# Mixer's first chunks in another order, S5 tables on POOL, the last branch rows kept in SBUF, and routing with one scan

## The chip, the cores and the metric

The kernel runs on one core of a Trainium2 chip. Time is that of the device, in microseconds (us), from the start to the end of one execution. An engine name in the text is PE (matrix products), DVE (vector), ACT (activation functions), POOL (GpSimd) or SP (it issues most DMAs).

## What is computed

One decoder layer on 2048 tokens of 1024 features: a normalisation, a mixer of four causal branches that are merged with gates, a residual, a second normalisation, a mixture of experts (32 experts in 4 groups, two per token), a residual and a last normalisation.

```python
def hybrid_mixer(xn, w_in, ...):
    proj = xn @ w_in                                   # 2048 x 1792
    ya = short_conv_mixer(a_b, a_c, a_x, conv_a_w)     # bg * conv3(cg * xv)
    yb = pool_mixer(p_u, pool_w, pool_b, pool_scale)   # window means of 2, 4, 8, 16 tokens, then a product
    yc = s5_mixer(s_u, ...)                            # h_t = a h_(t-1) + B u_t, complex; gelu; glu
    yd = rglru_mixer(l_x, l_g, ...)                    # conv4, two gates, h_t = a_t h_(t-1) + b_t
    branch = jnp.einsum('bskw,kwd->bskd', stack(ya, yb, yc, yd), branch_w)
    gates = jax.nn.sigmoid(xn @ merge_gate_w + merge_gate_b)
    return jnp.sum(gates * branch, axis=2) @ w_out

def hier_moe(xn, ...):
    # softmax over 4 groups, best group; the two best of its 8 experts; their softmax times the group's value
    # tokens sorted by expert, blocks of rows per expert
    h = jax.nn.silu(xb @ w1[e]) * (xb @ w3[e])
    return h @ w2[e]                                   # weighted, added to the token's row

def reference(x, ...):
    h = x + hybrid_mixer(rms_norm(x, norm1_g), ...)
    h = h + hier_moe(rms_norm(h, norm2_g), ...)
    return rms_norm(h, final_norm_g)
```

## The kernel before

Every large product is made from splits: a float32 operand is written as a high part (`_hi`, by ACT) and a low part (`_lo`, by DVE or POOL), and three matmuls per tile take hi·hi, lo·hi and hi·lo. The program runs in stages: mixer (`mix_branches`), merge (`merge_branches`), routing (`route`), experts (`run_experts`), and the final sum (`combine`). Within a stage each engine has its own list of instructions written out by hand in the order in which it runs; engines wait for one another on semaphores. There is no scheduler. What an engine does next is what stands next in its list, so an instruction that waits holds up all behind it.

**Mixer.** Four chunks of 512 tokens. For each, ACT squares and scales the rows of x (`squares`, `scale_rows`), DVE computes the inverse root by Newton steps in between (`rms_scale`, which calls `rsqrt_steps`), PE transposes (`first_tiles`), ACT and DVE write the two halves of the transposed x (`x_highs`, `x_lows`). Then fourteen projection tiles (`tile(c, i)`) of 24 matmuls give the inputs of the branches, in the order of `F_ORDER`. The two PSUM rings `gr` (emptied by ACT, `evac`) and `dr` (emptied by DVE) hold the tiles' results and those of the small products: `gates` (the block-diagonal gates of the RG-LRU branch, on `xc` of `lru_conv`), `pool_out` (on the pooled rows of `pool_mix`; `pool_result` empties it), `states_in` and `states_out` (the S5 branch: input to states, states to output), and `glu`. DVE's pieces are `lru_conv`, `gate_poly`, `lru_squares`, `lru_out`, `conv_a(c, j)` (the short convolution), `states(c, u)`, `y_poly`, `y_gelu`, `carry_states` and `glu_out`. The buffer `late` holds in chunk 0 the raw weights `raw` and later the states and the S5 output; so `tile(2, 0)`'s loads and the store of a branch go through SP's one queue.

In chunk 0 w_in is also split: SP loads a raw tile, ACT writes `win_hi` and POOL `win_lo`, and both are spilled to DRAM (`w_in_parts`) to be loaded in the later chunks. The rows of `u` make a round trip through DRAM (`turn_u`, on POOL) to `u4`. DVE prepares parameters during that time (lines 988 to 1110; the semaphore `masks_set` closes it), POOL then builds tables of cosines and sines by doubling (lines 439 to 450), and DVE the powers of the S5 matrices (lines 1124 to 1138), which PE transposes into Toeplitz tables.

At its end SP stores the chunk's four branches and x to DRAM. **Merge** loops over four trips of 512 tokens, and the last chunk comes first: `load_piece` and `load_x_parts` load branches and x again. SP loads for the next trip after the current one is split. `load_merge_weights` brings one set of weights per branch.

**Routing.** On DVE: softmaxes, one-hot marks (`oh`, `hot`) of the chosen experts, counts by PE (`tri`, `ones`), running sums over the 16 token tiles, blocks per expert, positions (`pos`), and the table of tokens for each block (`table`). Beside it POOL splits expert 0's weights into low parts (lines 1776 and 1781 of `ExpertWeights`).

**Experts.** For each block of tokens POOL gathers rows (`gather`), PE transposes them, and the three products follow. Weights of the next expert are loaded by SP, split into high parts by ACT and low parts by DVE and POOL while the current expert runs.

## Time and profile before

| | |
|---|---|
| time, median of 3 runs | 2833.48 us (2831.18 to 2833.7) |
| profiled execution | 2833.71 us |
| its span in the profile | 2832.1 us |
| PE busy / DVE / ACT / POOL | 2423.3 / 1457.3 / 1034.9 / 563.8 us |
| mixer | 0 to about 570 us |
| merge | about 570 to 1768 |
| routing | 1768 to about 1847 |
| experts | 1847 to about 2700, then the sum |

The profiled execution took 1.6 us more than its span, that is time around the first and last instruction. Busy time is summed over instructions; a stage in which PE is busy most of the time is bound by matmul work, a stage in which it is not is bound by what PE waits for. In a timeline row the bracket holds how long the engine was idle before the group, and who released it: an engine and line, or a DMA by its tensors, where "DVEq" or "SPq" is the engine's sequencer. In a window row the busy times of PE, PE's weight loads, DVE, ACT and POOL stand in this order.

### The profile page before, as it was taken

To read this page: it belongs to the slowest core of one execution; us is meant where nothing else is said; L and a number is where in the kernel's file an instruction comes from. 1 tells how busy PE (TensorE), PEld (TensorE's weight loads), DVE (VectorE), ACT (ScalarE), POOL (GpSimd) and SP (SyncE) were. 2 spreads that over 40 slices of the span, in tenths; PEclk is the share of its full clock that TensorE was granted. 3 is DMA by queue.
4 is the path that set the end of the run, shared out by engine and by line. 5 is a ranking of instruction groups with operands and counts; after the bars stand their busy time and mean duration, and the time that the engine had idled before them with its cause. 6 is when DMAs were issued, how large, how long until landed. Compare 5 with 4: busy or idle time off the path is not lost. (4 is left out here: it accounts for less than half of the span.)

```text
span 2832.1 us, 36678 instructions
## 1 busy us (share of the span) xinstructions
PE 2423.3 (86%) x11820; PEld 1866.0 (66%) x11821; DVE 1457.3 (51%) x2190; ACT 1034.9 (37%) x1254; POOL 563.8 (20%) x436
## 2 busy tenths in 40 slices
PE   6678698879999999999999999189999999998930
PEld 5466476668857886688758875167777667777730
DVE  6777366533333343334334333846456564665648
ACT  4322232222222222122212221146556565666621
POOL 3501001000000000000000000434334443345451
PEclk9889899989999999899999998589999999999975
DMA  8653456564463446244624452277777777788866
GB/s 251 250 190 115 164 201 244 156 210 136 129 208 100 125 142 209 81 143 135 209 90 134 129 185 107 90 257 297 265 270 286 276 255 267 276 308 319 295 259 282
DMA packets 385018, 569.61 MB, mean 201 GB/s; under 512 B 34896, under 2 KB 218448, under 8 KB 384976
## 3 DMA queue, kind: packets, MB, share of 16 engines
q1 hardware_dynamic: 348416, 462.89, 47.7%
q0 software_dynamic: 24624, 84.96, 8.1%
q10 hardware_dynamic: 11936, 21.24, 2.0%
q8 instruction: 21, 0.34, 0.1%
q14 instruction: 21, 0.17, 0.0%
HBM read 445.54 MB, written 123.47 MB: 201 GB/s over the span
## 5 line engine op out<-in xcount | busy, mean ns | idle before, releaser
L1424 PE MATMUL mrgps<-xn_hi,w_hi 128*128 128x512 f32 x1024 | 403.2, 394 | 20.9 <-DVE w_lo L1493 20.9
L1424 PE MATMUL mrgps<-xn_lo,w_hi 128*128 128x512 f32 x1024 | 402.2, 393 | 0.0
L1424 PE MATMUL mrgps<-xn_hi,w_lo 128*128 128x512 f32 x1024 | 401.7, 392 | 0.0
L1781 POOL TENSOR_TENSOR w_lo<-w_raw,w_hi 128x1024 fp32r<-128x1024 f32 x128 | 326.9, 2588 | 241.3 <-ACT w_hi L1772 241.3
L1776 DVE TENSOR_TENSOR w_lo<-w_raw,w_hi 128x2048 fp32r<-128x2048 f32 x124 | 303.3, 2487 | 34.6 <-ACT w_hi L1767 34.6
L1493 DVE TENSOR_TENSOR w_lo<-w_raw,w_hi 128x1280 fp32r<-128x1280 f32 x129 | 192.5, 1492 | 127.8 <-ACT w_hi L1358 126.1
L1375 ACT ACTIVATE gt<-mrgps,mb 128x512 f32<-128x512 f32 x128 | 88.2, 689 | 447.4 <-PE mrgps L1424 447.4
L1909 PE MATMUL exps<-w_hi,xT_hi 128*128 128x256 f32 (+1 forms) x768 | 247.7, 323 | 1.9 <-DVE xT_lo L2101 1.9
L1909 PE MATMUL exps<-w_lo,xT_hi 128*128 128x256 f32 (+1 forms) x768 | 245.7, 320 | 0.0
L1909 PE MATMUL exps<-w_hi,xT_lo 128*128 128x256 f32 (+1 forms) x768 | 245.7, 320 | 0.0
L1339 POOL DMA_DIRECT2D expert_rows<-zeros x32 | 29.5, 923 | 1061.5 <-DVE w_lo L1493 1008.1
L1767 ACT ACTIVATE w_hi<-w_raw 128x2048 fp32r<-128x2048 f32 x128 | 237.8, 1906 | 3.6 <-DMA w_raw<-in_expert_w_dram 3.6
L1358 ACT ACTIVATE w_hi<-w_raw 128x1280 fp32r<-128x1280 f32 x129 | 164.5, 1275 | 201.5 <-DVE tmp L1514 135.2
L1424 PEld LDWEIGHTS mrgps<-xn_hi,w_hi 128*128 128x128 f32 x1024 | 194.9, 190 | 63.1 <-issue 22.2
L1444 PE MATMUL mrgps<-wout,merged 128*128 128x512 f32 x512 | 222.1, 593 | 6.7 <-DVE merged L1516 6.7
L1514 DVE SCALAR_TENSOR_TENSOR tmp<-gt,mrgps 128x512 f32<-128x512 f32 x96 | 66.0, 688 | 302.1 <-PE mrgps L1424 302.1
L1424 PEld LDWEIGHTS mrgps<-xn_lo,w_hi 128*128 128x128 f32 x1024 | 194.7, 190 | 40.4
L1424 PEld LDWEIGHTS mrgps<-xn_hi,w_lo 128*128 128x128 f32 x1024 | 194.5, 190 | 40.6
L662 PE MATMUL mixps<-xn_hi,win_hi 128*128 128x512 f32 x448 | 185.7, 414 | 40.2 <-DVEq L916 12.9
L662 PE MATMUL mixps<-xn_lo,win_hi 128*128 128x512 f32 x448 | 179.3, 400 | 0.0
L662 PE MATMUL mixps<-xn_hi,win_lo 128*128 128x512 f32 x448 | 178.9, 399 | 0.0
L1444 PEld LDWEIGHTS mrgps<-wout,merged 128*128 128x128 f32 x512 | 96.3, 190 | 125.1 <-issue 116.7
(393 smaller groups left out, 4117.9 us busy)
## 6 DMA issues: line engine op xcount, KB each, us to landing
w_raw<-in_expert_w_dram SPq DMA_DIRECT2D x128, 1024.0 KB, 8.7
w_raw<-in_merge_gate_w_dram SPq DMA_DIRECT2D x132, 512.0 KB, 4.1
w_raw<-in_expert_w_dram SPq DMA_DIRECT2D x32, 2048.0 KB, 14.4
expert_rows<-zeros POOLq DMA_DIRECT2D x32, 1008.0 KB, 7.3
win_hi<-w_in_parts SPq DMA_DIRECT2D x42, 512.0 KB, 3.9
win_lo<-w_in_parts SPq DMA_DIRECT2D x42, 512.0 KB, 5.4
w_raw<-in_branch_w_dram SPq DMA_DIRECT2D x132, 128.0 KB, 4.0
expert_rows<-ysb ACTq DMA_DIRECT2D x64, 256.0 KB, 2.8
```

Source lines behind the costliest of these rows:

```text
L662: last = pe.matmul(ring.bank(key)[:], w[:, n % NW, cols], x[:, k], start=(k + j == 0), stop=(k == KD - 1 and j == 2))
L1339: pool.dma_start(dram["y"][ds(i * FILL, FILL), :].rearrange("(p r) (q n) -> p (r q) n", r=2, n=256), zeros[:].unsqueeze(1).to_broadcast([F ...
L1358: act.activation(w_hi[:, k % 2].rearrange("p k n -> p (k n)"), w_raw[:, k].rearrange("p k n -> p (k n)"), ACT.Copy).then_inc(w_hi_set, 1)
L1375: act.activation(gt[:], gbank[k % 2][:], ACT.Tanh, scale=0.5, bias=mb[:, k, ds(d, 1)]).then_inc(g_free, 1)
L1424: last = pe.matmul(bank[:], w[:, k % 2, kk], x, start=(kk == w_tiles[0] and j == 0), stop=(kk == w_tiles[-1] and j == 2))
L1444: last = pe.matmul(bbank[h][:], merged[:, kk, t * P:(t + 1) * P], wout[:, kk, h * 512:(h + 1) * 512], start=(kk == 0), stop=(kk == KD - 1))
L1493: dve.tensor_tensor(lo, w_raw[:, k].rearrange("p k n -> p (k n)"), hi.bitcast(F32), ALU.subtract).then_inc(w_split, 1)
L1514: dve.scalar_tensor_tensor(tmp[:], gt[:], 1.0, bbank[k % 2][:], ALU.add, ALU.mult).then_inc(b_free, 1)
L1767: act.activation(self.hi13[:, i], self.raw13[:, i], ACT.Copy).then_inc(self.high13, 1)
L1776: eng.tensor_tensor(self.lo13[:, i], self.raw13[:, i], self.hi13[:, i].bitcast(F32), ALU.subtract).then_inc(self.split13, 1)
L1781: eng.tensor_tensor(self.lo2[:, f], self.raw2[:, f], self.hi2[:, f].bitcast(F32), ALU.subtract).then_inc(self.split2, 1)
L1909: last = pe.matmul(bank[:, 0:n], x[:, k], weights[:, 2 * w + k // 4, cols], start=(k + i == 0), stop=(k == KD - 1 and i == 2))
```

## The change

All stages but `combine` are touched, and `rsqrt_steps` is shared.

- `rsqrt_steps` makes three Newton rounds where it made four: three fewer dependent DVE instructions in each of its uses (4 in the mixer, 16 in merge, 8 in `combine`).
- Mixer, PE: in chunk 0 tiles 8 and 9 come ahead of the gates, and `pool_out(0)` goes behind tile 3 of chunk 1. In chunk 1 `pool_out(1)` goes from behind tile 11 to behind tile 9. In chunks 2 and 3 `states_out(c-1)` goes from ahead of the first tiles to behind tile 3; `states_in`, the gates and `glu(c-1)` come one or two tiles later.
- Mixer, DVE: `rms_scale(1)` comes ahead of `pool_mix(0)`, and `x_lows(1)` ahead of `conv_a(0)`. `pool_result(1)` comes ahead of `states(1)`. `conv_a(c, 1)` goes behind `x_lows(c+1)`. The powers are gone from DVE; POOL makes them, after its tables, into the same buffers.
- Mixer, POOL: the table doublings (seven times six instructions) are woven between the last seven weight splits. ACT squares chunk 1 into `su`, so it waits for the store of `u` and no longer for `lru_out`. Three raw buffers remain of four, and the block-diagonal weights live in a spare part of `w_raw`, so that SP loads the fourth set of merge weights only after `pool_out(3)`.
- Hand-over: a buffer `branch_rows`, allocated outside both stages, holds the branches of each chunk. Those of chunk 3, and its x, are not stored and not loaded again; merge's first trip takes them from there.
- Routing: POOL no longer splits expert 0's weights there. One split stands on DVE ahead of the copy of the table, the other seven on POOL in `run_experts`, between the first gathers. The counts are laid out by expert, one scan with a mask (`later_tile`) gives the running sums in place of 15 additions, and a shift gives the number of blocks in place of a comparison with 30 thresholds. The matmul for the totals goes ahead of that for the ranks, and the first gather is issued in `route`.
- Experts: DVE waits for POOL's part of the next expert's splits (`split13`) before its own.

```diff
```diff
 
     s.link(dve.tensor_scalar(y.bitcast(I32), mean_sq.bitcast(I32), -0.5, 1597463007.0, ALU.mult, ALU.add))
     s.link(dve.tensor_scalar(half, mean_sq, -0.5, None, ALU.mult))
-    for _ in range(4):
+    for _ in range(3):
         s.link(dve.tensor_tensor(t, y, y, ALU.mult))
         s.link(dve.tensor_tensor(t, t, half, ALU.mult))
         s.link(dve.scalar_tensor_tensor(y, t, 1.5, y, ALU.add, ALU.mult))
@@ -127,7 +127,7 @@
...
-                if i == 7:
+                if i == 5:
                     sp.wait_ge(t_full, KD)
                     load_x(1)
-                if i == 9:
+                if i == 10:
                     store_xT(0)
...
+            dr.filled(sp, ("pool", CH - 1, 1))
+            load_merge_weights(sp, io, w_raw, merge_w_in, NBR - 1, 0)
+            sp.wait_ge(xT_out, 32 * (CH - 1))
             for b in range(NBR):
-                sp.wait_ge(ys_out[b], 16 * CH)
+                sp.wait_ge(ys_out[b], 16 * (CH - 1))
```
```
On POOL (the powers that follow on it are the same instructions as the removed ones of DVE):
```diff
```diff
+            for i in range(NF):
+                pool.wait_ge(w_high, i + 1)
+                pool.tensor_tensor(w_lo[:, i % NW], raw[i % NR], w_hi[:, i % NW].bitcast(F32), ALU.subtract).then_inc(w_split, 1)
+                if i == 6:
+                    pool.wait_ge(unit_rot, 2)
+                if i >= 6 and i - 6 < CC.bit_length() - 1:
+                    double_tables(2 ** (i - 6))
+                if i == 8:
+                    write_u(pool, 0)
             assert ts.n == 6 * (CC.bit_length() - 1)
+            read_u(pool, 0)
+            ts.settle()
+            pool.wait_ge(masks_set, 1)
...
             def squares(c):
                 for t in range(Q):
+                    room = lru[:, t // 2, 2 * (t % 2):2 * (t % 2) + 2, :]
+                    if c == 1:
+                        act.wait_ge(sq_done, Q + t)
+                        room = su[:]
                     act.wait_ge(x_in[t], c * 16 + 16)
-                    act.activation(lru[:, t // 2, 2 * (t % 2):2 * (t % 2) + 2, :].rearrange("p a b -> p (a b)"), xin[:, t], ACT.Square,
+                    act.activation(room.rearrange("p a b -> p (a b)"), xin[:, t], ACT.Square,
                                    accum_out=ssq[:, t:t + 1]).then_inc(sq_done, 1)
```
```
On PE:
```diff
```diff
             pe.wait_ge(consts, 3)
             first_tiles(0)
-            for i in range(2, 8):
+            for i in range(2, 10):
                 tile(0, i)
             pe.wait_ge(par_in, 16 * len(params))
             pe.wait_ge(bd_in, 16 * 12)
             gates(0)
-            tile(0, 8)
-            tile(0, 9)
...
+            pool_out(1)
             states_in(1, 0)
             tile(1, 10)
             states_in(1, 1)
-            tile(1, 11)
-            pool_out(1)
-            tile(1, 12)
-            tile(1, 13)
+            for i in range(11, NF):
+                tile(1, i)
             glu(0)
...
             for c in range(2, CH):
-                states_out(c - 1, 0)
-                states_out(c - 1, 1)
                 first_tiles(c)
                 tile(c, 2)
                 tile(c, 3)
+                states_out(c - 1, 0)
+                states_out(c - 1, 1)
+                tile(c, 4)
+                tile(c, 5)
                 states_in(c, 0)
-                tile(c, 4)
+                gates(c)
                 states_in(c, 1)
-                tile(c, 5)
-                gates(c)
                 tile(c, 6)
                 tile(c, 7)
+                tile(c, 8)
                 glu(c - 1)
-                tile(c, 8)
+                tile(c, 9)
                 if c == CH - 1:
                     states_out(c, 0)
                     states_out(c, 1)
-                tile(c, 9)
                 tile(c, 10)
```
```
On DVE:
```diff
```diff
             lru_conv(0)
             gate_poly(0)
             lru_squares(0)
+            rms_scale(s, 1)
             pool_mix(0)
             lru_out(0)
+            x_lows(1)
             conv_a(0, 0)
-            rms_scale(s, 1)
             conv_a(0, 1)
             pool_result(0)
-            x_lows(1)
-            for k in range(2, -1, -1):
...
             carry_states(0)
+            pool_result(1)
             states(1, 0)
             states(1, 1)
-            pool_result(1)
             rms_scale(s, 2)
             conv_a(1, 0)
-            conv_a(1, 1)
             glu_out(0)
 
...
             for c in range(2, CH):
-                x_lows(c, (0, 1))
-                y_poly(c - 1, 0)
-                x_lows(c, (2,))
-                y_poly(c - 1, 1)
-                x_lows(c, (3, 4))
-                y_gelu(c - 1, 0)
-                x_lows(c, (5,))
-                y_gelu(c - 1, 1)
-                x_lows(c, (6, 7))
+                x_lows(c)
+                conv_a(c - 1, 1)
...
                     glu_out(c - 1)
                     rms_scale(s, c + 1)
                 conv_a(c, 0)
-                conv_a(c, 1)
+            conv_a(CH - 1, 1)
             glu_out(CH - 1)
```
```
Merge and routing:
```diff
```diff
             for c in range(PIECES):
-                load_piece(TRIPS - 1, c)
+                sp.sem_inc(act_in[c], 16)
                 sp.sem_inc(xp_in[c], 32)
...
-                    load_piece(m, c)
+                    load_piece(nxt, c)
                 sp.wait_ge(b_full, m * BPER + KD * SU)
                 for c in range(2):
-                    load_x_parts(m, c)
+                    load_x_parts(nxt, c)
...
-            pool.affine_select(out=tri[:], in_=ones[:], compare_op=ALU.is_gt, fill=0.0, base=0,
-                               pattern=[[1, P]], channel_multiplier=-1).then_inc(consts, 1)
-            for i in range(4):
-                wt.write_low13(pool, 0, i)
-            wt.write_low2(pool, 0)
+            pool.affine_select(out=below[:], in_=minus[:], compare_op=ALU.is_ge, fill=0.0, base=0,
+                               pattern=[[-1, P]], channel_multiplier=1).then_inc(consts, 1)
+            pool.wait_ge(later_ones, 1)
+            pool.memset(later[:, :, 0:1], 0.0).then_inc(consts, 1)
+            pool.wait_ge(table_set, 1)
+            wt.gather(pool, dram, table[:, 0:1], 1)
...
             dve.wait_ge(ranks, 1)
-            s.link(dve.tensor_copy(tot[:].rearrange("p t e -> p (t e)"), tot_ps[:]))
-            s.link(dve.memset(cum[:, 0], 0.0))
-            for i in range(1, TT):
-                s.link(TTc(cum[:, i], cum[:, i - 1], tot[:, i - 1], ALU.add))
-            s.link(TTc(cnt[:], cum[:, TT - 1], tot[:, TT - 1], ALU.add))
-
-            s.link(TTc(big[:], cnt[:].unsqueeze(2).to_broadcast([P, E, NSTEP]), io_over[:].unsqueeze(1).to_broadcast([P, E, NSTEP]), ALU.is_gt))
-            s.link(dve.tensor_reduce(nb[:], big[:], AX.X, ALU.add))
+            s.link(dve.memset(e1[:], 1.0))
+            s.link(dve.tensor_tensor_scan(cum[:].rearrange("p e t -> p (e t)"), later[:].rearrange("p e t -> p (e t)"), tot_ps[:], 0.0, ALU.mult, ALU.add))
+            s.link(dve.tensor_scalar(nb[:], cum[:, :, TT - 1], float(P), float(HB - 1 - P), ALU.max, ALU.add))
+            s.link(dve.tensor_copy(steps[:], nb[:]))
+            s.link(dve.tensor_scalar(steps[:], steps[:], HB.bit_length() - 1, None, ALU.logical_shift_right))
+            s.link(dve.tensor_copy(nb[:], steps[:]))
             s.link(dve.tensor_scalar(nb[:], nb[:], 1.0, None, ALU.add))
-            s.link(dve.memset(e1[:], 1.0))
...
+            wt.write_low13(dve, 0, 0)
             dve.wait_ge(tab_ready, 1)
-            s.link(dve.tensor_copy(table[:], tab_ps[:, 0:NBT]))
+            dve.tensor_copy(table[:], tab_ps[:, 0:NBT]).then_inc(table_set, 1)
```
```
Experts:
```diff
```diff
-            gather(0)
             pool.memset(ident[:], 0.0).then_inc(idz, 1)
             pool.wait_ge(idz, 1)
             pool.affine_select(out=ident[:], in_=ident[:], compare_op=ALU.not_equal, fill=1.0, base=0,
                                pattern=[[-1, P]], channel_multiplier=1).then_inc(idn, 1)
+            wt.write_low13(pool, 0, 1)
+            wt.write_low13(pool, 0, 2)
             gather(1)
+            wt.write_low13(pool, 0, 3)
+            wt.write_low2(pool, 0)
             over_blocks(pool, half_block, one)
...
                 gate(g)
                 if nxt is not None:
+                    dve.wait_ge(wt.split13, nxt * 4)
+                    dve.sem_inc(passed, 1)
                     wt.write_low13(dve, nxt, 0)
```
```

How the order of instructions changes at three places. A number in a name's line is the line of that kernel; "x2" is a run of equal instructions.

On DVE in chunk 0, after `lru_squares(0)` (lines 865 to 871 before). Before:
```order
L866 TENSOR_TENSOR lq<-lq,lg 128x512
L865 TENSOR_SCALAR lq<-lq 128x512
L866 TENSOR_TENSOR lq<-lq,lg 128x512
L871 SCALAR_TENSOR_TENSOR lru<-lru 128x512 x2
L894 TENSOR_TENSOR pw<-pu 64x512
L895 TENSOR_TENSOR pw<-pu 64x526
L896 TENSOR_TENSOR pw<-pw 64x512
L904 TENSOR_TENSOR pw<-pw,corr 128x16
```
After, the same place:
```order
L887 TENSOR_TENSOR lq<-lq,branch_rows 128x512
L892 SCALAR_TENSOR_TENSOR lru<-lru 128x512 x2
L855 TENSOR_SCALAR msq<-ssq 128x4
L97 TENSOR_SCALAR rst<-msq 128x4
L98 TENSOR_SCALAR rhalf<-msq 128x4
L100 TENSOR_TENSOR rtmp<-rst 128x4
L101 TENSOR_TENSOR rtmp<-rtmp,rhalf 128x4
L102 SCALAR_TENSOR_TENSOR rst<-rtmp,rst 128x4
...
L102 SCALAR_TENSOR_TENSOR rst<-rtmp,rst 128x4
L915 TENSOR_TENSOR pw<-pu 64x512
L916 TENSOR_TENSOR pw<-pu 64x526
```
The root of chunk 1's scale (12 instructions on 128x4) now stands between `lru_squares(0)` and the pool mixing.

On POOL, from the last mask of routing to the first two gathers (`xg`) of the experts. Before:
```order
L1612 AFFINE_SELECT tri<-ones 128x128
L1776 TENSOR_TENSOR w_lo<-w_raw,w_hi 128x2048 x4
L1781 TENSOR_TENSOR w_lo<-w_raw,w_hi 128x1024 x4
L1861 COPY idx<-table 128x1
L1864 DMA xg<-xn,idx 128x1024
L1875 MEMSET x_ident 128x128
L1877 AFFINE_SELECT x_ident<-x_ident 128x128
L1861 COPY idx<-table 128x1
L1864 DMA xg<-xn,idx 128x1024
```
After:
```order
L1612 AFFINE_SELECT below<-minus 128x128
L1615 MEMSET later_tile 128x32
L1758 COPY idx<-table 128x1
L1761 DMA xg<-xn,idx 128x1024
L1877 MEMSET x_ident 128x128
L1879 AFFINE_SELECT x_ident<-x_ident 128x128
L1783 TENSOR_TENSOR w_lo<-w_raw,w_hi 128x2048 x2
L1758 COPY idx<-table 128x1
L1761 DMA xg<-xn,idx 128x1024
L1783 TENSOR_TENSOR w_lo<-w_raw,w_hi 128x2048
L1788 TENSOR_TENSOR w_lo<-w_raw,w_hi 128x1024 x4
```
The first gather comes ahead of all splits, and the splits of expert 0 lie around the second one.

On DVE in routing, from the counts to the number of blocks. Before:
```order
L1695 COPY tot<-rtps 128x512
L1696 MEMSET cum 128x32
L1698 TENSOR_TENSOR cum<-cum,tot 128x32 x15
L1699 TENSOR_TENSOR rt_c<-cum,tot 128x32
L1701 TENSOR_TENSOR big<-rt_c,io_over 128x960
L1702 TENSOR_REDUCE rt_c<-big 128x32
L1703 TENSOR_SCALAR rt_c<-rt_c 128x32
L1704 MEMSET rt_c 128x32
L1705 SCALAR_TENSOR_TENSOR rt_c<-rt_c 128x32
```
After:
```order
L1695 MEMSET rt_c 128x32
L1696 SCALAR_TENSOR_TENSOR cum<-later_tile,rtps 128x512
L1697 TENSOR_SCALAR rt_c<-cum 128x32
L1698 CAST rt_steps_needed<-rt_c 128x32
L1699 TENSOR_SCALAR rt_steps_needed<-rt_steps_needed 128x32
L1700 CAST rt_c<-rt_steps_needed 128x32
L1701 TENSOR_SCALAR rt_c<-rt_c 128x32
L1702 SCALAR_TENSOR_TENSOR rt_c<-rt_c 128x32
L1703 MEMSET ends 128x1
L1704 CAST ends<-rt_c 128x32
L1705 TENSOR_SCALAR rt_c<-rt_c 128x32
L1707 TENSOR_TENSOR off<-rtps,cum 128x512
```
Fifteen additions and the two operations on 960 elements are replaced by one scan on 512 elements and a few on 32.

## Rows read from the trace of the kernel before

**Rows 1.** Windows, chunks 2, 3: us; PE, PEld, DVE, ACT, POOL busy; clock; DMA
```profile
317.97:439.34 121.37, 105.59 (x468) 83.17 (x469) 68.79 (x125) 38.73 (x56) 8.08 (x14) 0.93 0.61 222
439.34:562.07 122.73, 106.19 (x468) 82.32 (x468) 69.35 (x117) 31.58 (x47) 12.86 (x23) 0.94 0.62 201
```
**Rows 2.** Timeline 73 to 99; start, length, engine, line, idle before in brackets
```profile
74.18 6.98 POOL L432 TENSOR_TENSOR win_lo<-late,win_hi 128x1024 fp32r<-128x1024 f32 x3
...
73.30 8.03 DVE L1083 TENSOR_SCALAR vec<-vec 128x2 f32<-128x2 f32 x3
...
90.65 6.15 PE L701 MATMUL mixps<-xc,bd 128*128 128x512 f32 x8 [15.43 <-DVE xc L851]
...
98.37 0.40 PE L662 MATMUL mixps<-xn_lo,win_hi 128*128 128x512 f32 x1
98.60 0.39 PE L662 MATMUL mixps<-xn_hi,win_lo 128*128 128x512 f32 x1
```
**Rows 3.** Timeline 133 to 160, POOL's table doublings and DVE
```profile
134.24 0.61 POOL L444 TENSOR_TENSOR late<-tcos 128x256 f32<-128x256 f32 x1
...
135.74 2.14 DVE L928 SCALAR_TENSOR_TENSOR pw<-va,cwa,pw 128x512 f32<-128x512 f32 x2
...
149.52 1.54 DVE L928 SCALAR_TENSOR_TENSOR pw<-va,cwa,pw 128x512 f32<-128x512 f32 x2
...
154.26 1.41 DVE L843 SCALAR_TENSOR_TENSOR xn_lo<-mixps,g,xn_hi 128x512 fp32r<-128x512 f32 x2 [0.24 <-DVE pooled L915]
```
**Rows 4.** Windows: pool_mix(0), lru_out(0), powers, conv_a(1,1)
```profile
101.36:113.40 12.04, 12.04 (x57) 9.97 (x56) 11.49 (x14) 3.65 (x6) 5.27 (x2) 1.00 0.23 93
124.26:133.90 9.64, 7.16 (x32) 5.61 (x30) 9.36 (x13) 0.48 (x1) 9.09 (x12) 1.00 0.60 220
...
167.53:185.10 17.57, 15.62 (x69) 12.58 (x67) 16.59 (x43) 3.37 (x4) 0.75 (x1) 1.00 0.85 315
...
299.75:304.10 4.35, 3.21 (x16) 3.22 (x17) 4.21 (x7) 4.13 (x4) 0.00 (x0) 0.53 0.00 0
```
**Rows 5.** Timeline of ACT, squares of chunk 1
```profile
133.93 1.06 ACT L469 ACTIVATE lru<-w_raw 128x1024 f32<-128x1024 f32 x1 [9.18 <-DVE lg L882]
```
**Rows 6.** Timeline of PE in chunks 1 and 2, and of SP's queue
```profile
274.52 0.77 PE L662 MATMUL mixps<-xn_hi,win_hi 128*128 128x512 f32 x1 [9.50 <-DVEq L916]
...
317.97 0.79 PE L662 MATMUL mixps<-xn_hi,win_hi 128*128 128x512 f32 x1 [8.97 <-DMA win_lo<-w_in_parts]
...
353.49 3.78 PE L715 MATMUL mixps<-u,BT 128*128 128x128 f32 x16 [8.12 <-DMA u<-s_inputs]
...
336.51 11.11 SPq L357 DMA_DIRECT2D w_raw<-in_x_dram  x4
```
**Rows 7.** Timeline, end of the mixer: PE and SP's queue
```profile
545.87 0.48 PE L662 MATMUL mixps<-xn_hi,win_hi 128*128 128x512 f32 x1 [3.40 <-DVEq L916]
...
565.53 0.37 SPq L366 DMA_DIRECT2D branches<-late  x1
569.73 0.93 SPq L1275 DMA_DIRECT2D act_raw<-branches  x2
```
**Rows 8.** Timeline of DVE, six linked 2-element instructions
```profile
63.91 1.14 DVE L109 SCALAR_TENSOR_TENSOR bgcg<-bgcg 128x2 f32<-128x2 f32 x6
```
**Rows 9.** Timeline of routing: POOL, DVE, PE
```profile
1779.54 18.81 POOL L1776 TENSOR_TENSOR w_lo<-w_raw,w_hi 128x2048 fp32r<-128x2048 f32 x4 [10.09 <-ACT w_hi L1767]
...
1779.70 4.91 DVE L1663 TENSOR_TENSOR oh<-io_e,rt_ei 128x512 f32<-128x512 f32 x1
...
1803.77 6.75 DVE L1698 TENSOR_TENSOR cum<-cum,tot 128x32 f32<-128x32 f32 x15
...
1814.10 0.69 DVE L1709 TENSOR_TENSOR off<-rtps,cum 128x512 f32<-128x512 f32 x1
...
1791.51 1.91 PE L1641 MATMUL rtps<-hot,ones 128*128 128x512 f32 x2
```
**Rows 10.** Timeline of DVE, a weight split of expert 1
```profile
1881.00 4.22 DVE L1776 TENSOR_TENSOR w_lo<-w_raw,w_hi 128x2048 fp32r<-128x2048 f32 x1 [1.12 <-ACT w_hi L1767]
```

278 lines of the change are left out of this document (133 added, 145 removed).

## Prediction

> **What bounds the kernel now.** I cut the span into stages at the first matmul of each mixer chunk. In chunk 2 PE is busy 105.6 of 121.4 us, in chunk 3 106.2 of 122.7 [rows 1]; chunks 0 and 1, with the stops named next, are looser. The matmul work itself is left alone by this change. Reordering can only win idle time, so I read who is waited for. (1) PE stops for 15.43 us at the chunk 0 gates, waiting for DVE's `xc`, and behind that stop lies POOL: one operation of DVE's preparation shows 8.03 us for three 2-element instructions exactly while POOL does three weight splits in 6.98 us [rows 2]. (2) In chunk 1 PE waits 9.50 us for line 916, the pool result that DVE does only after the S5 states; before chunk 2 it waits 8.97 us for `win_lo`, which is loaded into memory that `glu_out(0)` frees late; inside chunk 2 it waits 8.12 us for `u` [rows 6]. (3) At the mixer's end the last branch store is issued at 565.53 and the first loads of the merge only at 569.73 [rows 7]. (4) In routing DVE is the path, and POOL's four splits (18.81 us) and four more slow it: an operation on 512 elements that takes 0.69 alone shows 4.91 beside them [rows 9].
>
> **Chunk 0: about nothing.** Four splits of w_in still precede the masks, and DVE's wait for them stays. Thirty small table doublings now lie between the splits. POOL's own cost of one is 0.61 on 256 elements [rows 3] and less on the early, smaller ones; that DVE preparation also shares time with them. I put the masks about 4 us later (bounds −1 and +7: no overlap, and every doubling in DVE's way). In exchange tiles 8 and 9 now stand ahead of the gates, inside the 15.43 us stop. Before, the gates end at 96.8, and tiles 8 and 9 follow from about 98, each 24 matmuls that start 0.23 us apart [rows 2], 5.6 us: tile 10 starts at 109.4. Now the first `xc`, ready at 90.65, comes 4 us later with the masks and 1.7 more for POOL's last splits, which slip onto its operations: 96.4; the second, 3 us of work alone, I put at 101. The gates are then done by 104, the mask transposes follow, and tile 10 starts at about 105, 4.5 earlier. ACT's root of chunk 0 ended at 124.7, 9.18 us before the squares of chunk 1, which waited for DVE's `lg` [rows 5]. It now ends at 120.2, and the squares, 4.2 us for four, no longer wait: 124.4.
>
> From there DVE is the path. The order below lets it do rms_scale(1) first (12 instructions at 0.19 alone [rows 8] and 0.3 more each beside table work [rows 3]: 5.9), then pool_mix(0) and lru_out(0), 12.04 and 9.64 us [rows 4], plus 2.4 for about a dozen table operations more beside them (line 928 shows 2.14 beside POOL, 1.54 alone, for two, so up to 0.3 each [rows 3]; those windows hold some of it already), 24.1 together. That gives 154.4 for the first `x_lo` of chunk 1; before it is 154.26 [rows 3]. **Gain 0**, bounds −5 and +5. The squares come 14 us earlier and win nothing, since x_lows stands behind the same DVE work.
>
> **Chunk 1: −10.5.** The powers (17.57 us, 42 operations [rows 4]) leave DVE, but conv_a(0) and pool_result(0), some 10.7 us, take their place, and PE's own tiles 0 to 3 last as long as before; only 0.5 is won up to the Toeplitz tables. POOL does the powers from about 117 on; at its 0.61 for an operation of this size [rows 3] they take 26 us, and PE asks for them near 183. pool_result(1) now stands ahead of the states, so PE's 9.50 us wait [rows 6] goes. With 0.5 for smaller waits: −10.5 at the end of glu(0).
>
> **Start of chunk 2: −15.5.** The loads of its weights wait for the store that glu_out(0) feeds. conv_a(1,1) (4.35 us [rows 4]) is no longer ahead of glu_out, and rms_scale is three links shorter: six links show 1.14, so 0.19 each, 0.6 [rows 8]. 10.5 + 4.35 + 0.6 = 15.5. The 8.97 us wait itself stays: store, issue and landing all follow each other as before.
>
> **Chunk 2: −2.7 more.** states_out(1) moves from ahead of the tiles to behind tile 3: +5.4 of PE work, so 111.0. The idle 15.8 [rows 1] should fall to 7.7: the wait for `u` (8.12) loses its reason, but SP's x loads, which occupied it for 11.11 us [rows 6], stand ahead of later weights, and I leave 3.0 for tile 5; and tile 9 now waits for a buffer that ACT empties only behind lru_root, 4.7. 111.0 + 7.7 = 118.7 against 121.4.
>
> **Chunk 3: −0.1.** Again +5.4 for states_out(2) and +4.7 for the root. New are 3.6 in front of pool_out, since the pool branch comes after two y polynomials, and 4.6 at tile 12 in place of 3.40 [rows 7]. What goes is the wait for `u`, short stops, and 1.5 of restarts at the lower clock. 106.2 − 1.5 + 5.4 + 4.7 + 3.6 + 4.6 = 123.0, or nothing won. Glu(3) ends **18.3 earlier** than in the trace. If none of the new waits appears it is 35; if all the old ones are refilled it is 4.
>
> **Boundary: −4.5.** The branches of chunk 3 stay in SBUF: no landing wait between the store and the merge (about 3.5 of 569.73 − 565.53), and two issues of together 0.93 less ahead of SP's parameter loads [rows 7]. The weights of the fourth branch are now loaded after pool_out(3), well before they are used. **Merge: −2.3**: the norms at the end of each trip lose three links; I count one norm per trip on the path, 4 × 0.585, bounds 0 and 16 × 0.585 = 9.4. Sum so far −25.1.
>
> **Routing: −27.6.** Without POOL beside it `oh` and `hot` take 0.69 each from 1779.70: `hot` is there at 1781.1 instead of 1789.5. Line 1641's two passes take 1.9 [rows 9] and now come first, so totals are there at 1783.3; the small softmax operations (0.2 each alone) fit in that time. The scan of 512 elements replaces 15 adds (6.75) and two operations on 960 elements (1.16 and 1.15, lines 1701 and 1702 of the trace). I take 1.3 for it, between 0.69 for a plain operation and twice that; eight operations of about 0.2 follow. `off` then starts at 1786.5 instead of 1814.10 [rows 9]. The rest is unchanged. Sum −52.7.
>
> **Experts: +2.6.** This work is not gone. The gather is issued 0.7 us earlier, but POOL's eight splits of expert 0 now run beside expert 0. They end at about 1868.4, some 2 us after its first products need them, and the load of the second matrix of expert 1 is issued later; the DVE split at 1881.00 shows 4.22 instead of some 2.3 beside POOL [rows 10], and such meetings become more. Bounds 0 and +10. DVE's new wait on the splits stands behind a wait for ACT's `w_hi` of 1.1 and queues only that split. **Combine: −0.6**, one rsqrt at its end. Total **−50.7**.
>
> The profiled execution took 2833.71; its median is 2833.48. 2833.7 − 50.7 = 2783.0, and on the median's basis 2782.8: 2783.
>
> A rule speaks against moving the powers. The rows show DVE at 2.14 beside POOL's table work and 1.54 alone, 0.3 for one operation [rows 3]. The Trainium skill, page "SBUF — State Buffer", section "SBUF: two separate sides", says that the port pair which DVE and GpSimd share is an exclusive lock, held for a whole instruction, while the other one fully blocks. With that rule the 8.03 us of rows 2 agree, and the 0.3 of line 928 only half. By that rule each of POOL's operations could hold DVE for its whole length, and the sum would be about 7 us less good; that is rival B.
>
> **The rivals.**
> A, the forecast: 2775 to 2791. Chance 0.58.
> B, every POOL operation in chunk 0 holds DVE for its full 0.61: 24 of them lie beside x_lows and the convolutions, 24 × 0.3 more = +7, to +12: 2791. For it: 8.03 us for three tiny operations [rows 2]. Against: line 928's rows show only half. 0.12.
> C, expert 0's splits are late and expert 1's loads stay behind: +8, 2791. For it: nothing hides these splits; against: experts keep several pieces in store. 0.10.
> D, later chunks refill every wait (DVE is as long as before there): the mixer gives 4 and not 18.3: 2797. 0.08.
> E, the new waits in chunks 2 and 3 don't appear: −17, 2766. 0.08.
> F, slower: POOL's powers become the bound. PE waits for them near 183 and POOL begins near 117, so 66 us are there for 42 operations: it costs from 1.56 us each, and eats the whole gain of 50.7 from about 2.75 each. Row 134.24 shows 0.61 [rows 3]; at 3 us the powers end 60 us late: 2844. 0.02.
> G, nothing measurable: the splits moved out of routing cost the experts all that routing gains, and the mixer refills. 0.02.
>
> **The numbers.** 0.2% (5.7 us) is about what a measurement of this kernel can tell from no change. A to E are all faster by more. The range must leave out at most 0.2: 2768 reaches nearly to E, and 2802 takes in B, C and D with the bounds of the experts. Faster 0.96, same 0.02, slower 0.02.
>
> **What would show it.** Right: `off` starts about 6.8 us after the `oh` of row 1779.70 instead of 34.4, and `hot` takes 0.69; first `x_lo` of chunk 1 at 154 ± 5; glu(0) ends near 281, chunk 2 starts near 302, chunk 3 near 421, glu(3) ends near 544; no PE wait for L916's successor in chunk 1; a new stop of about 4.7 us before tile 9 in chunks 2 and 3; POOL's powers near 0.6 each. Wrong: DVE operations at over 1 us beside POOL in 95 to 160 (B); PE waiting for POOL's `w_lo` in the first two experts (C); a wait for `u` or `win_lo` of 8 us in chunks 2 and 3 (D).

## The result and the profile after

The changed kernel takes 2790.39 us (median of 4 runs, 2788.01 to 2791.28) where the kernel before takes 2833.59 in the same comparison. The ratio is 0.9844, with a 95% interval of 0.9827 to 0.9861: 43 us less, where 50.7 less were forecast (2783). The profiled execution has a span of 2789.7 us, 42.4 less than that of before. Shifts and stages that follow are counted in spans of profiled executions, one for each kernel. Nine of the traces below have the same program up to the first `x_lo` of chunk 1, and there they differ: chunk 0's masks end between 82.5 and 84.5, that `x_lo` begins between 144.6 and 147.1 (the changed kernel's 144.74 is near the early end). A difference of up to 2.5 us between two traces at one such place shows nothing by itself.

The two traces can be laid side by side at places that both have. For each place, the shift in the trace against the shift that the prediction gives up to there:

| place | before | after | shift | forecast |
|---|---|---|---|---|
| first `x_lo` of chunk 1 (DVE) | 154.26 | 144.74 | −9.5 | 0 |
| end of glu(0) (PE) | 291.7 | 270.4 | −21.3 | −10.5 |
| first tile of chunk 2 | 317.97 | 291.50 | −26.5 | −15.5 |
| first tile of chunk 3 | 439.34 | 421.37 | −18.0 | −18.2 |
| end of glu(3) | 562.1 | 554.1 | −8.0 | −18.3 |
| first product of merge | 573.00 | 561.14 | −11.9 | −22.8 |
| first operation of routing (DVE) | 1768.08 | 1749.72 | −18.4 | −25.1 |
| `off` | 1814.10 | 1768.16 | −45.9 | −52.7 |
| first transposes of the experts (PE) | 1847.3 | 1797.6 | −49.7 | −53.4 |
| third group of transposes | 1885.9 | 1847.3 | −38.6 | −50.1 |
| last transposes of the experts | 2711.8 | 2675.0 | −36.8 | −50.1 |
| end of the span | 2832.1 | 2789.7 | −42.4 | −50.7 |

The stage windows of chunks 2 and 3 answer [rows 1]. Columns as there: length, then PE, its weight loads, DVE, ACT and POOL, the granted clock, DMA.

```profile
291.50:421.37 129.87, 106.96 (x468) 84.19 (x469) 69.70 (x124) 39.07 (x56) 8.09 (x14) 0.89 0.56 203
421.37:554.10 132.73, 114.62 (x516) 89.54 (x516) 73.94 (x123) 32.29 (x47) 12.99 (x23) 0.91 0.48 152
```

Before, chunk 2 took 121.37 and chunk 3 122.73 us; now 129.87 and 132.73. In chunk 3 some 5.4 us of `states_out` came into the window (516 matmuls for 468). In chunk 2 the number stays at 468: `states_out(1)` came in and `states_out(2)` went out. PE's idle time grew from 15.8 to 22.9 us in chunk 2 and from 16.5 to 18.1 in chunk 3; the rest is work at a lower granted clock (0.89 for 0.93 of full speed in chunk 2, 0.91 for 0.94 in chunk 3). What PE waits for between 290 and 556 us, summed (engine and line waited for, us in total, times, longest):

```profile
PE mixps L686 <- ACT pu L538: 19.6, 2, 9.8
PE mixps L686 <- DMA win_lo<-w_in_parts: 18.7, 3, 9.9
```

The waits for `u` (8.12 us in [rows 6]) are gone, as the change meant, and three waits of about 10 us each stand in their place: one for weights in chunk 2 (9.87) and one for the pool tiles in each of chunks 2 and 3 (9.78 and 9.79). The first of both kinds, in the timeline of PE, with ACT's timeline around the second:

```profile
340.08 0.79 PE L686 MATMUL mixps<-xn_hi,win_hi 128*128 128x512 f32 x1 [9.87 <-DMA win_lo<-w_in_parts]
375.89 0.77 PE L686 MATMUL mixps<-xn_hi,win_hi 128*128 128x512 f32 x1 [9.78 <-ACT pu L538]
...
373.09 0.63 ACT L559 ACTIVATE lq<-lq 128x512 f32<-128x512 f32 x1 [15.44 <-DVE lq L887]
...
374.69 1.99 ACT L538 ACTIVATE pu<-mixps 128x512 f32<-128x512 f32 x2
```

ACT empties the two pool tiles (line 538) only at 374.69, behind `gate_tanh` (line 559), for which it waited 15.44 us on DVE's gate polynomials; they stand behind the S5 states, which now start later, since `states_in` has moved back.

Routing answers [rows 9]. DVE's and PE's timeline:

```profile
1761.45 0.69 DVE L1663 TENSOR_TENSOR oh<-io_e,rt_ei 128x512 f32<-128x512 f32 x1
1762.17 0.69 DVE L1685 TENSOR_TENSOR hot<-oh 128x512 f32<-128x512 f32 x1
...
1765.26 1.22 DVE L1696 TENSOR_TENSOR_SCAN cum<-later_tile,rtps 128x512 f32<-128x512 f32 x1
...
1768.16 1.01 DVE L1707 TENSOR_TENSOR off<-rtps,cum 128x512 f32<-128x512 f32 x1
...
1763.01 2.05 PE L1640 MATMUL rtps<-hot,ones 128*128 128x512 f32 x2 [14.32 <-DVE hot L1685]
```

`oh` and `hot` take 0.69 us, where `oh` took 4.91; `off` begins 6.7 us after `oh` and not 34.4. The start of the experts answers [rows 10], in the timelines of POOL, DVE and PE:

```profile
1808.50 4.57 POOL L1783 TENSOR_TENSOR w_lo<-w_raw,w_hi 128x2048 fp32r<-128x2048 f32 x1
1813.02 9.32 POOL L1788 TENSOR_TENSOR w_lo<-w_raw,w_hi 128x1024 fp32r<-128x1024 f32 x4
...
1813.30 11.20 DVE L1783 TENSOR_TENSOR w_lo<-w_raw,w_hi 128x2048 fp32r<-128x2048 f32 x1 [2.90 <-ACT w_hi L1774]
...
1813.13 0.39 PE L1915 MATMUL exps<-w_hi,xT_hi 128*128 128x256 f32 x1 [2.67 <-POOL w_lo L1783]
1824.88 0.69 PE L1904 MATMUL exps<-x_ident,hg 128*128 128x128 f32 x2 [7.23 <-DVE hg L2095]
```

Here the splits that left routing come back: one DVE split, which takes 2.3 us where POOL is idle, lasts 11.20 us, and PE stops 2.67 us for a POOL split and 7.23 us for `hg`, which stands behind that DVE split.

### The profile page after: what moved, and what is told of

The parts are those of the page before. It is cut to its first block and busy times, and to the rows that moved or that the text cites. A ratio compares the mean times of both kernels' runs of the same rounds, so it can differ in the third digit from the quotient of the medians.

```text
span 2789.7 us, 36559 instructions
## 1 busy us (share of the span) xinstructions
PE 2422.9 (87%) x11820; PEld 1863.1 (67%) x11821; DVE 1414.7 (51%) x2050; ACT 1035.6 (37%) x1254; POOL 591.8 (21%) x479
## 5 line engine op out<-in xcount | busy, mean ns | idle before, releaser
L1783 DVE TENSOR_TENSOR w_lo<-w_raw,w_hi 128x2048 fp32r<-128x2048 f32 x125 | 314.5, 2557 | 36.5 <-ACT w_hi L1774 36.3
L686 PE MATMUL mixps<-xn_hi,win_hi 128*128 128x512 f32 x448 | 188.5, 421 | 69.6 <-DVE xn_lo L864 22.9
```

The lines of the kernel that those rows point to most:

```text
L686: last = pe.matmul(ring.bank(key)[:], w[:, n % NW, cols], x[:, k], start=(k + j == 0), stop=(k == KD - 1 and j == 2))
L1783: eng.tensor_tensor(self.lo13[:, i], self.raw13[:, i], self.hi13[:, i].bitcast(F32), ALU.subtract).then_inc(self.split13, 1)
```

## Experiments

Each run was compared anew with the kernel before, which took 2832.2 to 2833.9 us in these comparisons.

### Chunks 2 and 3: is the new order worth it?

Three edits ask what made the new stops. `e_evac` changes ACT's order only:

```diff
                 lru_gates(c)
-                gate_tanh(c)
                 for i in (6, 7):
                     evac(c, i)
+                gate_tanh(c)
                 lru_root(c)
```

> The changed kernel, with one edit in chunks 2 and 3 on ACT: the two pool tiles (evac 6 and 7) are emptied ahead of gate_tanh, which waits for DVE's gate polynomials behind the states. In the changed kernel PE stops 9.78 us before tile 8 in chunk 2 and 9.79 in chunk 3 for these two. Theory 1, the stops are the cost of the new order: both go and nothing takes their place, glu(3) ends 19.5 us earlier (534.6), time about 2771. Theory 2, DVE's chain is the bound behind them (the store that glu_out(1) feeds releases tile 13's weights, and pool_out waits for DVE in chunk 3): 6 us in chunk 2 and 4 in chunk 3 come back, time about 2780. Theory 3, PE's stops are refilled one to one: 2790.

Measured: 2778.6 us (2774.18 to 2784.09), ratio to before 0.9808 (0.9791 to 0.9825). Glu(3) ends at 540.9, 13.2 us earlier than in the changed kernel, 6.4 of it by the end of glu(1). That lies between the theories: the stop is real, and part of it is replaced at once. PE's timeline shows by what:

```profile
339.72 0.80 PE L686 MATMUL mixps<-xn_hi,win_hi 128*128 128x512 f32 x1 [9.05 <-DMA win_lo<-w_in_parts]
377.71 3.78 PE L764 MATMUL mixps<-branch_rows,glw 128*128 128x512 f32 x4 [4.47 <-ACT cg L540]
...
360.73 1.11 ACT L538 ACTIVATE pu<-mixps 128x512 f32<-128x512 f32 x1 [3.14 <-PE mixps L686]
...
373.02 0.63 ACT L559 ACTIVATE lq<-lq 128x512 f32<-128x512 f32 x1 [5.76 <-DVE lq L887]
```

ACT now empties the first pool tile at 360.73 and the second 5.4 us later, as PE delivers them, ahead of `gate_tanh` (373.02), and the next stop is 4.47 us for tile 8 (`cg`), which ACT empties behind `lru_root`. This is the wait that the prediction had, at 4.7 us, only one place earlier: ahead of glu(1) and not of tile 9. It was hidden behind a longer one.

`e_spx` changes SP's order only:

```diff
-                    if i == 4 and c + 1 < CH:
-                        store_xT(c)
-                        load_x(c + 1)
                     if i == 5:
                         store(3, c - 1, yd_full, lg)
+                    if i == 6 and c + 1 < CH:
+                        store_xT(c)
+                        load_x(c + 1)
```

> The changed kernel, with SP's store of the transposed x and its load of the next x moved behind the weights of tiles 5 and 6 in chunks 1 and 2. Theory 1, the 9.87 us stop at tile 5 of chunk 2 is made of this traffic standing ahead of tile 5's weights: it goes, and states, gates and DVE's chain come 9 us earlier, time about 2781. Theory 2, the traffic only moves, and tiles 6 to 8 wait for weights instead: PE's idle in chunk 2 changes by under 3 us, time 2787 to 2791. In both the x of chunk 3 still comes early enough, since ACT asks for it some 80 us later.

Measured: 2777.69 us (2775.24 to 2780.49), ratio 0.9802 (0.9785 to 0.9818). Theory 1: `states_in` of chunk 2 starts at 336.8 for 347.7, and glu(3) ends 12.1 us earlier. SP's queue in the changed kernel and in this one:

```profile
310.53 10.90 SPq L357 DMA_DIRECT2D w_raw<-in_x_dram  x4
321.53 1.21 SPq L353 DMA_DIRECT2D win_hi<-w_in_parts  x1
...
315.29 0.32 SPq L353 DMA_DIRECT2D win_hi<-w_in_parts  x1
...
320.74 0.32 SPq L353 DMA_DIRECT2D win_hi<-w_in_parts  x1
...
322.69 12.35 SPq L357 DMA_DIRECT2D w_raw<-in_x_dram  x4
```

In the changed kernel the load of x occupies the queue for 10.90 us, and the next weights are issued at 321.53 behind it. With the edit two more pairs of weights (315.29, 320.74) go ahead of it.

`e_old23` puts chunks 2 and 3 back into the order of before, on PE, ACT and DVE, with all else as in the changed kernel:

```diff
-                first_tiles(c)
-                tile(c, 2)
-                tile(c, 3)
                 states_out(c - 1, 0)
                 states_out(c - 1, 1)
-                tile(c, 4)
-                tile(c, 5)
+                first_tiles(c)
+                tile(c, 2)
+                tile(c, 3)
                 states_in(c, 0)
...
```

> The changed kernel with chunks 2 and 3 in the order of the kernel before on PE, ACT and DVE (states_out ahead of the first tiles, x_lows woven with the polynomials, conv_a(c,1) behind conv_a(c,0)); all else as changed. Theory 1, the new order of chunks 2 and 3 costs what the trace says, 18.5 us more for them than before, with 4.4 given for their earlier start: glu(3) ends near 540 where the changed kernel has 554, time about 2776. Theory 2, these chunks lose because something else of the change (the hand-over buffer, three raw buffers) makes weights or DVE late: the loss stays, time 2788 to 2794.

Measured: 2775.02 us (2770.19 to 2776.43), ratio 0.9783 (0.9767 to 0.98). Glu(3) ends at 539.5, where 540 was expected. So the part of the change that reorders chunks 2 and 3 costs about 15 us by itself; the change is faster in spite of it. `e_order` then asks whether the new order is bad or only unfinished. It has the edits of `e_spx` and `e_evac`, and empties tile 8 ahead of `gate_tanh` as well:

```diff
                 lru_gates(c)
-                gate_tanh(c)
-                for i in (6, 7):
+                for i in (6, 7, 8):
                     evac(c, i)
+                gate_tanh(c)
                 lru_root(c)
-                evac(c, 8)
```

> The changed kernel with two edits in its chunks: SP's store of x and load of the next x behind the weights of tiles 5 and 6, and ACT empties tiles 6, 7 and 8 ahead of gate_tanh and lru_root. One edit alone gave 13.2 us at glu(3), the other 12.1. Theory 1, two separate waits: the gains add, less what is common; the stop of 4.47 us before glu that came behind the first edit goes too: glu(3) ends near 530, time near 2765. Theory 2, both edits uncover the same bound, DVE's chain from the states to glu_out: glu(3) stays at 538 to 542, time 2774 to 2779, and the order of the kernel before (2775) is as good as the new one can get.

Measured: 2768.64 us (2763.91 to 2771.46), ratio 0.9768 (0.9752 to 0.9785). Glu(3) ends at 534.5, 19.6 us earlier than in the changed kernel. The waits of PE between 290 and 556 us:

```profile
PE mixps L685 <- DMA win_lo<-w_in_parts: 11.4, 3, 7.4
PE mixps L685 <- ACT su L582: 7.3, 2, 4.4
```

The 19.6 us of waits for `pu` are gone, those for weights fell from 18.7 to 11.4, and 7.3 for `su` (from glu) are what comes next. The gains of the two edits alone were 13.2 and 12.1, 25.3 together; the run that has both, and tile 8's edit besides, wins 19.6, so at least 5.7 of it is common to them. Glu(3) ends 5.0 us earlier than with the old order (`e_old23`), but the intervals of the two ratios overlap, and `e_spx`'s edit was not tried with the old order.

### Chunk 0 and the powers

The prediction had chunk 0's masks 4 us later; they are 3.8 earlier. `e_noweave` takes the doublings out from between the splits:

```diff
-                if i == 6:
-                    pool.wait_ge(unit_rot, 2)
-                if i >= 6 and i - 6 < CC.bit_length() - 1:
-                    double_tables(2 ** (i - 6))
                 if i == 8:
                     write_u(pool, 0)
+            pool.wait_ge(unit_rot, 2)
+            for i in range(CC.bit_length() - 1):
+                double_tables(2 ** i)
```

> The changed kernel with POOL's table doublings in one piece behind all splits again, as before; the read of u stays behind them. In the changed kernel DVE has the masks at 83.5, before at 87.3, where I had forecast 91. Theory 1, the woven doublings space the splits, and so keep three of them from running in a row beside DVE's preparation: masks return to about 87, first x_lo of chunk 1 from 144.7 to about 148, time about +3, 2793. Theory 2, it is the read of u that left the row of splits (POOL waited 7.46 us for it before, and then ran three splits on end): masks stay at 83 to 84, tables end later by about 5 us, and beside them DVE's lru_conv gets faster; x_lo within 1 us of 144.7 or earlier, time 2789 to 2791.

Measured: 2792.33 us (2786.69 to 2795.91), ratio 0.9844 (0.9827 to 0.986). The masks end at 82.7 (83.5 with the doublings woven in, 82.5 to 84.5 in all nine traces that have them so), so the 30 doublings that I priced at 4 us cost them about 1 us or nothing. But the first `x_lo` of chunk 1 comes at 149.1, 4.4 later (2.0 later than the latest of the nine): the tables then run beside the pool mixing. Neither theory had both halves. `e_readu` moves the read of `u` back between the splits too, and the doublings stay in one piece behind them:

```diff
-                if i == 8:
+                if i == 7:
                     write_u(pool, 0)
+                    read_u(pool, 0)
...
-            read_u(pool, 0)
```

> The changed kernel with POOL's part of chunk 0 in the order of before: write and read of u behind split 7, doublings in one piece behind all splits (powers follow them on POOL). Against the run with the doublings in one piece, only the place of the read of u differs. Theory 1, the read was the cause of the late masks: POOL waits some 7 us in it, three splits run on end beside DVE's preparation, masks at 86 to 88 in place of 83. Theory 2, raw buffers or the loads set when POOL splits, and masks stay at 83 to 84. Time 2792 to 2798 in both.

Measured: 2792.61 us (2788.06 to 2795.24), ratio 0.9856 (0.984 to 0.9872). The masks end at 84.2, within the spread of the nine, so Theory 1 falls: the read of `u` alone does not bring them back to 87. The run is no full return to before, though. POOL does wait 7.2 us for the read, but two splits run on end behind it and not three; three raw buffers remain of four, which may be why. What such a row does to DVE stands in the timelines of DVE, before and in this run, and of POOL in this run (POOL's row of before is in [rows 2]):

```profile
73.30 7.89 DVE L1083 TENSOR_SCALAR vec<-vec 128x2 f32<-128x2 f32 x1
...
71.35 5.47 DVE L1111 TENSOR_SCALAR corr<-corr,wcol 128x16 f32<-128x16 f32 x1
...
72.09 4.69 POOL L443 TENSOR_TENSOR win_lo<-late,win_hi 128x1024 fp32r<-128x1024 f32 x2
```

The 8.03 us of [rows 2] are not three operations that meet one split each. The first of them, on 2 elements, lasts 7.89 and ends at 81.19, with the row of three splits (81.16); the other two take some 0.16 each. In `e_readu` one on 16 elements outlasts a row of two (76.82 and 76.78). Such a wait costs about what the splits would cost DVE one by one. So it is their number ahead of the masks that counts: 11 hold DVE before, 9 in the changed kernel. Why there are two fewer was shown by a run made for something else, `e_rsq4`:

```diff
-    for _ in range(3):
+    for _ in range(4):
...
-    RSQ = 11
+    RSQ = 14
```

> The changed kernel with four Newton rounds. Theory 1, my forecast's count: 0.6 in the mixer, 2.3 in merge, 0.6 in combine, so +3.5. Theory 2, DVE is the path in all of combine (its groups follow each other 10.83 us apart before, 10.25 now), so all eight count there: 4.7, and 2.4 in merge; +8.

Measured: 2803.52 us (2801.88 to 2806.21), ratio 0.9898 (0.9882 to 0.9914): one Newton round costs 13 us (11.4 in the spans), more than either theory. By places: 3.6 up to the end of glu(3), 3.9 in merge and routing, 5.2 in the final sum, and −1.3 in the experts. In chunk 0 DVE's timeline shows why. Before, then with four rounds in the changed kernel, each with POOL's timeline:

```profile
13.37 2.23 DVE L100 TENSOR_TENSOR rtmp<-rst 128x4 f32<-128x4 f32 x1
15.63 2.28 DVE L101 TENSOR_TENSOR rtmp<-rtmp,rhalf 128x4 f32<-128x4 f32 x1
17.95 0.16 DVE L102 SCALAR_TENSOR_TENSOR rst<-rtmp,rst 128x4 f32<-128x4 f32 x1
...
13.24 4.66 POOL L432 TENSOR_TENSOR win_lo<-late,win_hi 128x1024 fp32r<-128x1024 f32 x2 [9.78 <-ACT win_hi L464]
...
13.26 2.23 DVE L100 TENSOR_TENSOR rtmp<-rst 128x4 f32<-128x4 f32 x1
15.52 0.16 DVE L101 TENSOR_TENSOR rtmp<-rtmp,rhalf 128x4 f32<-128x4 f32 x1
15.71 2.27 DVE L102 SCALAR_TENSOR_TENSOR rst<-rtmp,rst 128x4 f32<-128x4 f32 x1
...
13.12 2.35 POOL L443 TENSOR_TENSOR win_lo<-late,win_hi 128x1024 fp32r<-128x1024 f32 x1 [9.66 <-ACT win_hi L487]
```

The fourth round of the very first root falls on POOL's first two weight splits. Two of its links, on 4 elements, take 2.2 to 2.3 us and not 0.16. With three rounds the root is done at 13.3, just before POOL starts, and ACT can scale the rows at 15.38 for 18.20. The first `x_lo` of chunk 0 is at 21.8 with three rounds and at 24.5 with four, the gates of chunk 0 at 89.0 and 92.2, the first `x_lo` of chunk 1 at 144.7 and 149.9. With four rounds 11 splits hold DVE ahead of the masks, as before, and the masks end at 86.9 (87.3 before, 83.5 in the changed kernel): the round accounts for 3.4 of their 3.8 us. So three links, priced by me at nothing there, bring 2.7 us at the start, 4.0 at the end of chunk 1's squares, and with those of chunk 1's root 5.1 at its first `x_lo`, more than half of chunk 0's surprise (against the latest of the nine traces it is 2.8). In the final sum the groups of line 2215 and 2223 follow each other (timeline of DVE, before and after):

```profile
2766.01 5.24 DVE L2215 SCALAR_TENSOR_TENSOR ch<-cy,wts,ch 128x1024 f32<-128x1024 f32 x4
2776.84 5.24 DVE L2215 SCALAR_TENSOR_TENSOR ch<-cy,wts,ch 128x1024 f32<-128x1024 f32 x4
...
2727.06 5.24 DVE L2223 SCALAR_TENSOR_TENSOR ch<-cy,wts,ch 128x1024 f32<-128x1024 f32 x4
2737.31 5.24 DVE L2223 SCALAR_TENSOR_TENSOR ch<-cy,wts,ch 128x1024 f32<-128x1024 f32 x4
```

10.83 us apart before, 10.25 after: 0.58 less each, which is three links at 0.19. The even spacing fits DVE as the path for every group.

`e_powdve` puts the 42 power operations back on DVE:

```diff
             pool_result(0)
+            for k in range(2, -1, -1):
+                are, aim = (t[:].unsqueeze(2).to_broadcast([P, NS, SJ]) for t in (ar, ai))
+                re, im = Bp[0][:, :, k + 1, :], Bp[1][:, :, k + 1, :]
+                s.mark(dve.tensor_tensor(pt1, re, are, ALU.mult))
...
             lru_conv(1)
```

> The changed kernel with the 42 operations for the powers back on DVE, between pool_result(0) and lru_conv(1). Theory 1, POOL's powers hold DVE less than they save: x_lo of chunk 1 comes 2 to 5 us earlier than 144.7 without them, but the 17.6 us stand ahead of the Toeplitz tables and states(0), so chunk 1 ends 8 to 12 later, time 2798 to 2802. Theory 2, the powers on POOL give nothing, since the Toeplitz tables wait for PE's tiles: glu(0) within 3 us of 270.4, time 2788 to 2793.

Measured: 2800.05 us (2794.99 to 2804.3), ratio 0.9879 (0.9862 to 0.9895). Theory 1, with larger numbers on both sides. The squares of chunk 1 end at 117.4, and the first `x_lo` comes 19.6 us later, at 137.0; in the changed kernel it is 29.3 us from 115.4 to 144.7. PE then waits for the powers:

```profile
186.11 3.77 PE L770 MATMUL mixps<-w_raw,m 128*128 128x128 f32 x16 [18.93 <-DVEq L1138]
```

The states start 12.8 us later (198.1 for 185.3), glu(3) ends 10.5 later. So POOL's powers hold DVE by 9.7 us there, and moving them is still worth some 10. POOL pays as well: its 42 operations take 37.5 us in the changed kernel, from 109.9 to 147.4, where the forecast had 26.

### The boundary

`e_reload` stores the branches of chunk 3 and loads them again:

```diff
+            store(3, CH - 1, yd_full, lg)
+            store(1, CH - 1, yb_full, pl)
+            store(0, CH - 1, ya_full, ya)
+            store(2, CH - 1, glu_done, yn)
...
-                sp.sem_inc(act_in[c], 16)
+                load_piece(TRIPS - 1, c)
```

> The changed kernel with the branches of chunk 3 stored at the mixer's end and loaded again at merge's start, as before. Theory 1, only the landing and the two issues were saved, as forecast: the first merge product comes 3.9 us later after glu(3) (10.9 for 7.0) and the second stop is unchanged, time +4. Theory 2, these loads also stood in the way of the parameters that the first gates wait for (the last of them landed 15.2 us after the first product before, 11.0 now): the second stop grows by some 4 us too, time +8.

Measured: 2797.11 us (2794.13 to 2800.41), ratio 0.9874 (0.9858 to 0.989). PE's first two stops in merge, with the loads and in the changed kernel:

```profile
562.35 0.79 PE L1426 MATMUL mrgps<-xn_hi,w_hi 128*128 128x512 f32 x1 [10.04 <-DVE w_lo L1495]
580.75 0.79 PE L1426 MATMUL mrgps<-xn_hi,w_hi 128*128 128x512 f32 x1 [8.85 <-DVE w_lo L1495]
...
561.14 0.79 PE L1422 MATMUL mrgps<-xn_hi,w_hi 128*128 128x512 f32 x1 [7.04 <-DVE w_lo L1491]
575.92 0.79 PE L1422 MATMUL mrgps<-xn_hi,w_hi 128*128 128x512 f32 x1 [5.30 <-DVE w_lo L1491]
```

Both grow, the first by 3.0, the second by 3.6, and the time by 6.7: Theory 2. Behind the second stop DVE waits for the last parameter, `rb`, before it can prepare the gates' bias, and with the loads in the way that ends 14.6 us after the first product, without them 11.0.

### The price of the splits of expert 0

`e_splitroute` puts POOL's seven splits back into routing:

```diff
+            for i in range(1, 4):
+                wt.write_low13(pool, 0, i)
+            wt.write_low2(pool, 0)
             pool.wait_ge(table_set, 1)
             wt.gather(pool, dram, table[:, 0:1], 1)
```

> The changed kernel with POOL's seven splits of expert 0 back in routing, ahead of the gather. Theory 1, the trade of the change: DVE's 512-element operations show 4 to 5 us beside them again and routing takes 17 to 22 us more (the scan in place of the 15 adds stays, worth some 9), expert 0 gets its 11 back: time 2797 to 2803. Theory 2, most of routing's gain is the scan and not POOL's absence: routing takes under 10 us more, time at 2790 or below.

Measured: 2796.05 us (2792.22 to 2801.6), ratio 0.9871 (0.9852 to 0.989). The mechanism is that of Theory 1, and the time is just below its range: the way from the end of PE's totals to `off` is 18.4 us longer, and expert 0 is 11.2 faster, as before the change. The timelines of DVE and POOL:

```profile
1764.25 4.38 DVE L1693 TENSOR_TENSOR rt_g<-rt_g 128x16 f32<-128x16 f32 x1
...
1779.90 2.26 DVE L1701 CAST rt_steps_needed<-rt_c 128x32 int32<-128x32 f32 x1
...
1764.06 13.46 POOL L1786 TENSOR_TENSOR w_lo<-w_raw,w_hi 128x2048 fp32r<-128x2048 f32 x3 [11.90 <-ACT w_hi L1777]
1777.48 9.24 POOL L1791 TENSOR_TENSOR w_lo<-w_raw,w_hi 128x1024 fp32r<-128x1024 f32 x4
```

Operations on 16 elements take 4.4 us, the length of one POOL split, and later ones on 32 elements 2.26, that of a small split. So of routing's 27.5 us, 18.4 come from the absence of POOL's seven splits. The other 9.1 are not the scan and the shift alone: before, eight splits stood there, in a row of 28.0 us for 22.7 here, so some 5 of them may belong to the eighth, which the change gave to DVE. No run separates the two. `e_dve2` gives one of the seven to DVE:

```diff
             dve.tensor_copy(table[:], tab_ps[:, 0:NBT]).then_inc(table_set, 1)
+            wt.write_low13(dve, 0, 1)
...
-            wt.write_low13(pool, 0, 1)
             wt.write_low13(pool, 0, 2)
```

> The changed kernel with the second weight split of expert 0 on DVE behind the copy of the table in routing, where DVE waits, instead of on POOL; POOL has two large and four small splits left. In the changed kernel expert 0 loses 11 us: PE stops 2.67 us for a POOL split and 7.23 us for DVE's hg, which stands behind a DVE split of 11.20 us that ran beside POOL's row of splits. Theory 1, the length of that POOL row holds DVE: the row ends 4.6 us sooner, the DVE split shows about 7, and 4.5 to 7 us come back (2784 to 2786). Theory 2, expert 0's weights are late from the DMA and ACT (the high parts), not from POOL: the stops stay, time 2789 to 2792.

Measured: 2787.86 us (2785.97 to 2789.64), ratio 0.9844 (0.9827 to 0.986), which the comparison can't tell from the changed kernel. In the trace the mechanism shows: from the first to the third group of transposes it is 45.8 us for 49.7, and the DVE split is shorter.

```profile
1809.24 8.23 DVE L1784 TENSOR_TENSOR w_lo<-w_raw,w_hi 128x2048 fp32r<-128x2048 f32 x1 [1.12 <-ACT w_hi L1775]
...
1805.90 9.42 POOL L1789 TENSOR_TENSOR w_lo<-w_raw,w_hi 128x1024 fp32r<-128x1024 f32 x4
```

It begins at 1809.24, POOL's row of four ends at 1815.3, and 2.2 later the split is done. In the changed kernel it begins at 1813.30, the row ends at 1822.3, and again it takes 2.2 from there. So here a DVE split waits for all that is left of the row of back-to-back POOL splits, not for the one that is running. But the gather's index copy on POOL, now beside a DVE split, lasts 2.18 us for 0.18, and takes back half of the 3.9 us won.

`e_best` has the order edits and all four larger splits on DVE:

```diff
             low_x(0, 1)
+            wt.write_low13(dve, 0, 2)
+            wt.write_low13(dve, 0, 3)
             over_blocks(dve, half_block, one)
```

> The changed kernel with the order edits of the run before (SP's x traffic behind tile 6's weights, ACT's tiles 6, 7 and 8 ahead of gate_tanh: 2768.6) and all four larger splits of expert 0 on DVE, two in routing, two in the wait for the first products; POOL keeps the four small ones. Theory 1, what held expert 0 was the length of POOL's row beside DVE: from the first transposes to the third group of transposes 49.7 us become 38.6 to 42, time 2758 to 2761. Theory 2, DVE's own splits now stand where its gate work was, and POOL's four small ones hold them: the stretch stays near 46 and the time near 2765.

Measured: 2766.43 us (median of 5, 2760.48 to 2773.21), ratio 0.9761 (0.9743 to 0.978). From the first to the third transposes 43.6 us, between the theories, and the time is near that of Theory 2: DVE's two splits last 14.25 beside POOL's row of 9.35.

```profile
1785.14 14.25 DVE L1783 TENSOR_TENSOR w_lo<-w_raw,w_hi 128x2048 fp32r<-128x2048 f32 x2
...
1785.69 9.35 POOL L1788 TENSOR_TENSOR w_lo<-w_raw,w_hi 128x1024 fp32r<-128x1024 f32 x4
```

Against `e_order` (2768.64) its own part isn't clear of the noise; against the changed kernel (0.9844) both are clearly faster, by some 0.8%. `e_best` has the lowest median of the versions measured.

## Why the prediction was right, and where its steps were not

The time lay in the range and the direction was right; the sum was 7.5 us too good, and that it came so near owes much to luck, as the terms show. Term by term, forecast and measured in the spans:

| step | forecast | measured |
|---|---|---|
| chunk 0, to the first `x_lo` of chunk 1 | 0 | −9.5 |
| chunk 1, to the end of glu(0) | −10.5 | −11.8 |
| to the start of chunk 2 | −5.0 | −5.2 |
| chunk 2 | −2.7 | +8.5 |
| chunk 3 | −0.1 | +10.0 |
| boundary, first product | −4.5 | −3.9 |
| second stop of merge | none | −4.1 |
| merge's norms | −2.3 | −2.4 |
| routing | −27.6 | −27.5 |
| experts | +2.6 | +9.1 |
| final sum | −0.6 | −5.6 |

Five terms stand within 1.3 us: chunk 1, the way to chunk 2, the boundary, the norms, and routing, whose scan I put at 1.3 us and which took 1.22. The norms' −2.4 is what is left of merge behind its second stop. The other terms partly cancelled (chunk 0, the second stop and the final sum came out 18.6 us better than forecast, chunks 2 and 3 and the experts 27.8 worse), so the good total is no proof of the parts.

**Chunk 0 (off by 9.5).** The step that failed is "I put the masks about 4 us later". The doublings cost DVE's masks about 1 us or nothing (`e_noweave`), and `rms_scale(0)` wasn't in the sum at all, though three links left it: beside POOL's splits they were worth 2.7 us at the start and 3.4 at the masks (`e_rsq4`). The forecast also took the 8.03 us of [rows 2] for three meetings of a small operation and a split; it is one operation that waited for a row of three. Downstream the step was right: from the end of chunk 1's squares to `x_lo` the forecast has 30.0 us, the trace 29.3.

**Chunks 2 and 3 (off by 11.2 and 10.1).** Two of the new waits were named and mis-sized. "I leave 3.0 for tile 5" was 9.87 us, because those weights stand behind the x traffic, which `e_spx` moved. The 4.7 us behind `lru_root` is true (4.47 in `e_evac`, one place earlier), but ahead of it stands a longer one for the same reason one step earlier: tiles 6 and 7 behind `gate_tanh`, 9.78. I had followed ACT's list from tile 8 back to the root and not on to the tiles ahead of it. Two steps of chunk 2's sum were wrong as well, against each other in part. It adds 5.4 us of work for `states_out(1)`, though `states_out(2)` leaves the window: PE was busy for 106.96 us and not 111.0. And its idle time of 7.7 is 3.0 + 4.7, which puts at nothing, without a reason, the 7.7 us of other idle time that [rows 1] leaves beside the wait for `u`: 22.9 were measured, 9.87 + 9.78 and 3.3 of other waits. In chunk 3 some 4.5 us more are PE's busy time (114.6 where I had 110.1), at a granted clock of 0.91 for 0.94, where the forecast had 1.5 us of work at the lower clock go. The tile behind the 9.79 us stop takes 8.4 us to the start of glu, at a mean granted clock of 0.64, between the two levels of 1.2 and 2.4 GHz; most others take 5.4 to 5.6:

```profile
491.88 0.76 PE L686 MATMUL mixps<-xn_hi,win_hi 128*128 128x512 f32 x1 [9.79 <-ACT pu L538]
...
500.30 1.88 PE L764 MATMUL mixps<-branch_rows,glw 128*128 128x512 f32 x4
```

This stop is paid twice, once in waiting and once in the lower clock after it. Rival D had the later chunks refill every wait, and its sign, a wait of 8 us for `win_lo`, came with 9.87; it was the right mechanism for these two chunks at a chance of 0.08, and the surplus of chunk 0 hid it in the total.

**Merge's second stop (−4.1).** I counted what the first stop waits for. The removed loads also stood ahead of the parameters that the second one waits for (`e_reload`).

**Experts (off by 6.5).** The lateness was named with 2.6 and rival C with 8; it was 11 in expert 0 and 13 over all, less the 3.8 won between `off` and the first transposes, where I had 0.7 for the earlier gather. Rival C's sign, PE waiting for a `w_lo` of POOL, came too (2.67). The term that failed is the collision: I took 4.22 for the DVE split, and it was 11.20. The 1.8 us lost behind expert 0 stay open; the new wait on `split13` was not tested alone.

**Final sum (off by 5.0).** "One rsqrt at its end" was wrong. All eight groups are DVE's path, 0.58 each, 4.7 together; the other 0.9 us lie ahead of the first group and are not explained.

**Rival B** did not decide the time, but its subject is real. POOL's powers held DVE by 9.7 us (`e_powdve`): over the 31 of them that ran between the squares and `x_lo` 0.31 each, the 0.3 of [rows 3] that the forecast used. Its sign, DVE operations of over 1 us beside POOL, showed in part: those that take 0.69 to 0.75 us alone took 0.88 to 1.28 in the pool mixing. The full 0.61 of rival B for each POOL operation did not show beside POOL's small operations. Beside its splits full waits did: 16-element operations took 4.4 us beside splits of 4.5, and three DVE splits and two small operations waited for a whole row. The Trainium skill, page "SBUF — State Buffer", section "SBUF: two separate sides", has the pair held for one instruction. DVE's small operations in routing agree with that. The 7.89 us of [rows 2], which the prediction counted as agreeing, the 5.47 in `e_readu` and the three splits do not: there the wait covered several POOL instructions.

## What to carry to other kernels

When an instruction list is reordered, walk back from each new wait over everything that stands ahead of it on the releasing engine's list, and price the longest, not the first you find; a wait removed elsewhere can uncover the next, as 9.8 us uncovered 4.5. Small dependent operations are worth what runs beside them: three links were worth 0.6 us alone and 2.7 beside two POOL splits, and work moved off one stage's path onto POOL is best put where DVE has nothing urgent for the whole length of POOL's row: here a split of 2.3 us waited 9.0, and an operation on 2 elements 7.7. Split a large change into its parts on the chip: here one part (the order of chunks 2 and 3) cost 15 us in a change that gained 43, and three short edits made good all of it.

## What the runs showed of the hardware

DVE splits on 128x2048 that met a row of ready POOL splits ended 2.2 us, their own length, after the whole row, in three kernels: 11.20 us long where the row ended 9.0 after the split's start, 8.23 for 6.1, and 12.05 for 9.9 (the first of the two in `e_best`), there with the DVE split begun 0.55 us ahead of the row. But the 4.22 us of [rows 10] is a split that got in between the third and the fourth POOL split, and held the fourth by as much. Why DVE is let in there and not in the other three stays open. Most operations on 2 to 32 elements beside POOL splits last what is left of the running one: 2.2 to 2.4 us beside splits of 2.4, 4.4 beside 4.5. Two did not: one on 2 elements took 7.89 us, to the end of a row of three splits (the kernel before), and one on 16 elements 5.47, to the end of a row of two (`e_readu`). Why these waited for the row stays open too. Beside POOL's powers, of 0.61 to 1.5 us each, DVE lost 0.31 for each.
